# A two-block transformer kernel on one core: a reordered opening, compression products woven between dense ones, and one modulation group moved to the output projection

## The reference, cut to what matters

```python
mod = silu(c) @ w_ada + b_ada                     # 2048 x 12288, one row
shift_m, scale_m, gate_m, shift_f, scale_f, gate_f = split(mod, 6)
h = rms_norm(x, pre_norm_mix) * (1 + scale_m) + shift_m
q, k_c, v_c, ... = split(h @ w_in, ...)
# compression: 32-token blocks of k_c and v_c, each 4096 values -> 128 -> silu -> 128
o = attention(...) @ w_o
x = x + gate_m * rms_norm(o, post_norm_mix)
h = rms_norm(x, pre_norm_ffn) * (1 + scale_f) + shift_f
```

## Time and profile before

| | us |
|---|---|
| median of 3 runs | 2958.68 |
| runs, lowest and highest | 2956.5, 2975.97 |
| the profiled execution | 2958.95 |
| its span, first to last instruction | 2956.8 |
| PE busy, share of the span | 2874.6, 97% |
| DVE busy | 1701.4, 58% |
| ACT busy | 1254.4, 42% |
| mean granted PE clock | 0.983 |

### The profile page before, as it was taken

How to read it: one execution, slowest core, us unless ns; L and a number is a source line. 1 busy time by engine, 2 the same in 40 slices (tenths; PEclk the granted TensorE clock), 3 DMA queues, 4 the chain that set the end, 5 groups by cost and what they waited for, 6 DMA issues and landing times.

```text
span 2956.8 us, 50977 instructions
## 1 busy us (share of the span) xinstructions
PE 2874.6 (97%) x22328; PEld 2652.0 (90%) x22328; DVE 1701.4 (58%) x1507; ACT 1254.4 (42%) x1197; POOL 130.3 (4%) x111
## 2 busy tenths in 40 slices
PE   6999999999999999999999999999999999999998
PEld 5899987799889997899999889999979998899887
DVE  7879877795444454455455654445745554455444
ACT  3334444444434543345343544443345443344333
POOL 0011110000000000000022320000000000000000
PEclk8799999999999999999999999999999999999999
DMA  9999778596556655655452016566554555565553
GB/s 360 388 317 305 268 238 297 176 368 225 186 198 188 197 190 180 203 191 175 157 168 66 10 45 199 187 197 221 178 185 159 197 187 197 187 197 189 181 194 119
DMA packets 300452, 596.72 MB, mean 202 GB/s; under 512 B 12144, under 2 KB 17776, under 8 KB 299760
## 3 DMA queue, kind: packets, MB, share of 16 engines
q1 hardware_dynamic: 294864, 587.83, 59.1%
q10 hardware_dynamic: 5408, 6.23, 0.8%
HBM read 583.80 MB, written 6.29 MB: 200 GB/s over the span
## 4 chain that ended last, share of the span: by engine, by line
PE 83%; DVE 8%; DMA 3%; ACT 3%; issue 2%; POOL 0%; SPq 0%; ACTq 0%; DVEq 0%
PE ps L2429 30%; PE ps L2352 26%; PE ps L2949 9%; PE ps L2534 4%; DVE ada_acc L1593 3%; PE ps L2549 3%; DVE wL L1373 2%; PE ps L3072 2%; DMA ada<-w_ada 2%; PE ps L2830 2%; ACT wH L770 1%; PE ps L2510 1%; DMA raw<-w_up 1%; PE ps L2375 1%; PE ps L2331 0%
## 5 line engine op out<-in xcount | busy, mean ns | idle before, releaser
L1373 DVE TENSOR_TENSOR wL<-raw,wH 128x2048 fp32r<-128x2048 f32 x436 | 1004.3, 2304 | 1064.1 <-ACT wH L770 1060.0
L770 ACT ACTIVATE wH<-raw 128x2048 fp32r<-128x2048 f32 x436 | 837.8, 1922 | 1277.7 <-PE ps L2429 475.4
L2429 PE MATMUL ps<-actH,wH 128*128 128x256 f32 x2816 | 779.3, 277 | 1.7 <-DVE wL L1373 1.6
L2429 PE MATMUL ps<-actL,wH 128*128 128x256 f32 x2816 | 777.7, 276 | 0.0
L2429 PE MATMUL ps<-actH,wL 128*128 128x256 f32 x2816 | 777.7, 276 | 0.0
L2429 PEld LDWEIGHTS ps<-actH,wH 128*128 128x128 f32 x2816 | 529.0, 188 | 3.9 <-DVE wL L1373 2.1
L2429 PEld LDWEIGHTS ps<-actL,wH 128*128 128x128 f32 x2816 | 529.0, 188 | 0.1
L2429 PEld LDWEIGHTS ps<-actH,wL 128*128 128x128 f32 x2816 | 528.9, 188 | 0.0
L2352 PE MATMUL ps<-wH,hidH 128*128 128x512 f32 x1024 | 403.4, 394 | 1.3 <-DVE wL L1373 1.3
L2352 PE MATMUL ps<-wH,hidL 128*128 128x512 f32 x1024 | 400.4, 391 | 0.0
L2352 PE MATMUL ps<-wL,hidH 128*128 128x512 f32 x1024 | 397.4, 388 | 0.0
(11 more groups left out here) (438 smaller groups left out, 3654.6 us busy)
## 6 DMA issues: line engine op xcount, KB each, us to landing
raw<-w_in SPq DMA_DIRECT2D x96, 1024.0 KB, 5.3
ada<-w_ada SPq DMA_DIRECT2D x80, 1024.0 KB, 8.3
raw<-w_up SPq DMA_DIRECT2D x64, 1024.0 KB, 5.4
raw<-w_down SPq DMA_DIRECT2D x64, 1024.0 KB, 5.1
raw<-w_mlp_up SPq DMA_DIRECT2D x64, 1024.0 KB, 5.2
raw<-w_mlp_down SPq DMA_DIRECT2D x64, 1024.0 KB, 5.0
raw<-w_gates SPq DMA_DIRECT2D x48, 1024.0 KB, 5.1
raw<-w_o SPq DMA_DIRECT2D x16, 1024.0 KB, 6.5
```

Of the source, the lines that this page charges most:

```text
L770: nc.scalar.activation(wH[:, s % SPLIT if L[name]["spg"] > 1 else r % SPLIT, :, :], raw[:, slot, :, :], ACT.Copy).then_inc(wh_ready, 1)
L1373: nc.vector.tensor_tensor(wL[:, b, :, :], raw[:, slot, :, :], wH[:, b, :, :].bitcast(F32), ALU.subtract).then_inc(wl_ready, 1)
L2429: ins = nc.tensor.matmul(out, w[:, b, k, cols], v[:, kk, :], start=(kk == 0 and j == 0 and n % 2 == 0), stop=(kk == STEP_K * spg - 1 and j ...
```

## The change

Opening: the squares are taken of the token layout, by ACT with a sum per token, so the root is of a 128x2 tile; PE turns `x` back with a diagonal of the reciprocal roots (32 products into four banks), and ACT copies the normalised `x_f` out. The transfer `gw` is issued after that. Coefficients of c = 1 and 2 are taken one block earlier. For c = 2 and 3 ACT writes `actH` straight from `x_f`, piece by piece, and DVE makes `actL` in four pieces. The first weight tile of quarter 3 is split in halves. `gate_part` goes ahead of the second `front_total`, with two products behind it whose result nobody reads. SP issues the first three weight tiles one block earlier, and tiles 9 to 12 after block 31.

Compression: 24 and 40 of the 64 products are spread between the dense products of steps (1,1) and (1,2). Modulation: group 15 moves from the attention part to `w_o` (32, 16 and 16 blocks).

```diff
-    WIN_ADA = [(2, 0, 0, 1), (1, 1, 3, 4), (1, 1, 0, 1)] + [(2, 1, 0, 1)] * 4 + [(2, 1, 0, 2)]
-    WO_ADA = [(0, 0, 0, 0), (1, 1, 1, 1), (1, 1, 0, 2), (2, 1, 1, 0)]
+    WIN_ADA = [(0, 0, 1, 2), (1, 1, 2, 2), (1, 1, 0, 1)] + [(2, 1, 0, 1)] * 5
+    WO_ADA = [(0, 0, 0, 0), (2, 2, 1, 1), (2, 1, 1, 2), (2, 1, 1, 0)]
...
 # SP
-                    if c == 0 and n >= 5:
-                        weight_block(n - 5)
+                    if c == 0 and n in (4, 5, 6):
+                        weight_block(n - 4)
...
-                    if c == 3 and n == 2:
-                        weight_block(FRONT * c)
+            weight_block(FRONT * 3)
             weight_block(FRONT * 3 + 1)
+            weight_block(FRONT * 3 + 2)
+            weight_block(FRONT * 3 + 3)
             sp.wait_ge(xT_out, 2 * (KT // GT))
...
 # ACT
+                if c == KT // GT - 1:
+                    act.wait_ge(xT_out, n + 1)
+                    chain(nc.scalar.activation(sq_tok[:, t, :], x[:, t, :], ACT.Square, accum_out=rms[:, 1, t:t + 1]))
+            nc.scalar.activation(rms[:, 0, :], rms[:, 1, :], ACT.Sqrt, bias=eps, scale=1.0 / D).then_inc(std_ready, 1)
+            act.wait_ge(low_part, 1)
+            for t in range(TT):
+                ins = nc.scalar.activation(rstd_d[:, t, :], ident, ACT.Identity, scale=rms[:, 2, t:t + 1])
+            ins.then_inc(high_part, 1)
+            for n in range(2 * (KT // GT)):
+                act.wait_ge(xT_done, 2 * (KT // GT) + n + 1)
+                nc.scalar.activation(flat(x_f[:, 2 * n:2 * n + 2, :]), ps[:, n % 4, :], ACT.Copy).then_inc(xT_out, 1)
+            act.wait_ge(xT_out, 4 * (KT // GT))
             act.dma_start(gw[:, :, :], matrix(a["w_gate"])).then_inc(gw_in, 16)
...
 # DVE
+                    if c == 0 and n == 5:
+                        dve.wait_ge(std_ready, 1)
+                        nc.vector.reciprocal(rms[:, 2, :], rms[:, 0, :]).then_inc(low_part, 1)
+                    if c and n == 0:
                         front_coefficients(c - 1)
+                        if c == 3:
+                            first_low(2)
+                            front_split(2, 0)
+                            rest_low(2)
...
+            last_half(slice(0, 2), low_part)
             front_coefficients(3)
+            first_low(3)
+            dve.wait_ge(wh_ready, FRONT * 3 + 1)
+            last_half(slice(2, 4), wl_ready)
+            rest_low(3)
...
 # PE
-                if c < 3:
-                    front_total(2 * c + 3)
                 if c == 0:
                     pe.wait_ge(gw_lo, 1)
                 ins = gate_part(c)
+                if c < 3:
+                    front_total(2 * c + 3)
+                if c < 3:
+                    unread(2)
...
-            compress(0, 22)
-            w_in_step(1, 1)
+            w_in_step(1, 1, compress_between(0, 24))
             pe.wait_ge(vtok_ready, 2)
             score(0)
-            compress(22, 43)
             ada_total(8, 3, 0)
-            w_in_step(1, 2)
-            compress(43, 64).then_inc(cmp_sum, 1)
-            ada_total(9, 3, 0)
+            w_in_step(1, 2, compress_between(24, 2 * CMP_LEN))
             w_in_step(1, 3)
```

More of the change, by code:

```diff
@@ L843, in token_squares @@
                 c = r + i * L.unroll(name)
+                if name == "w_o" and c == 0:
+                    act.wait_ge(ada_rows, 16)
                 for t in range(TT):
@@ L936, in _ @@
             act.wait_ge(consts_in, 48)
-            act.wait_ge(x_in, 16)
-            for c in range(KT // GT):
-                nc.scalar.activation(flat(sq[:, GT * c:GT * (c + 1), :]), flat(x_f[:, GT * c:GT * (c + 1), :]), ACT.Square
-                                     ).then_inc(sq_ready, 1)
-            act.wait_ge(ssum_ready, 1)
-            nc.scalar.activation(std[:, :], ps[:, 6, 0:T], ACT.Sqrt, bias=eps, scale=1.0 / D).then_inc(std_ready, 1)
             for n in range(2 * (KT // GT)):
@@ L957, in _ @@
             for c in range(KT // STEP_K):
+                if c >= 2:
+                    l = FRONT * c
+                    act.wait_ge(raw_in[l % RAW], 16 * (l // RAW + 1))
+                    act.wait_ge(step_done, l + 1)
+                    if c == 2:
+                        nc.scalar.activation(wH[:, l % SPLIT, :, :], raw[:, l % RAW, :, :], ACT.Copy).then_inc(wh_ready, 1)
+                    else:
+                        nc.scalar.activation(wH[:, l % SPLIT, 0:2, :], raw[:, l % RAW, 0:2, :], ACT.Copy).then_inc(high_part, 1)
+                        nc.scalar.activation(wH[:, l % SPLIT, 2:4, :], raw[:, l % RAW, 2:4, :], ACT.Copy).then_inc(wh_ready, 1)
+                    act.wait_ge(coef_ready, c + 1)
+                    act.wait_ge(act_ready, 2 * (c - 1))
+                    for k in range(GT):
+                        n = GT * c + k
+                        ins = nc.scalar.activation(actH[:, n, :], x_f[:, n, :], ACT.Identity, bias=mod[:, 0, n:n + 1],
+                                                   scale=cf(0)[:, n:n + 1])
+                        if k:
+                            ins = nc.scalar.activation(yf[:, c % 2, k, :], x_f[:, n, :], ACT.Identity, bias=mod[:, 0, n:n + 1],
+                                                       scale=cf(0)[:, n:n + 1])
+                        if k % 2:
+                            ins.then_inc(h_ready, 1)
+                        else:
+                            ins.then_inc(high_part, 1)
+                    act.sem_inc(y_ready, 2)
+                    front_split(c, 1)
+                    front_split(c, 2)
+                    continue
                 front_split(c, 0)
@@ L1649, in front_coefficients, with piece_low, first_low, rest_low @@
                                                ).then_inc(coef_ready, 1)
+            def piece_low(c, k):
+                n = GT * c + k
+                nc.vector.tensor_tensor(actL[:, n, :], yf[:, c % 2, k, :], actH[:, n, :].bitcast(F32), ALU.subtract
+                                        ).then_inc(act_ready if k % 2 else low_part, 1)
+            def first_low(c):
+                n = GT * c
+                dve.wait_ge(coef_ready, c + 1)
+                link(nc.vector.tensor_scalar(yf[:, c % 2, 0, :], x_f[:, n, :], cf(0)[:, n:n + 1], mod[:, 0, n:n + 1], ALU.mult, ALU.add))
+                dve.wait_ge(high_part, 2 if c == 2 else 5)
+                piece_low(c, 0)
+            def rest_low(c):
+                dve.wait_ge(h_ready, 2 * c + 1)
+                piece_low(c, 1)
+                dve.wait_ge(high_part, 3 if c == 2 else 6)
+                piece_low(c, 2)
+                dve.wait_ge(h_ready, 2 * c + 2)
+                piece_low(c, 3)
             for c in range(KT // STEP_K):
@@ L2447, in _ @@
             pe.wait_ge(consts_in, 48)
-            for _ in range(4):
+            for _ in range(2):
                 nc.tensor.matmul(ps[:, 4, :], ident, common[:, 0:4 * P], start=True, stop=True)
-            for c in range(KT // GT):
-                pe.wait_ge(sq_ready, c + 1)
-                for k in range(GT * c, GT * (c + 1)):
-                    ins = nc.tensor.matmul(ps[:, 6, 0:T], ones, sq[:, k, :], start=(k == 0), stop=(k == KT - 1))
-            ins.then_inc(ssum_ready, 1)
+            pe.wait_ge(x_in, 16)
             for n in range(2 * (KT // GT)):
```

147 lines of the change are left out of this document (84 added, 63 removed).

## The result

The changed kernel takes 2996.85 us (median of 4 runs, 2992.58 to 3007.91) against 2965.04 for the kernel before beside it: 1.0119 times as long, 95% interval 1.0100 to 1.0139 (the ratio on record; the quotient of these two medians is 1.0107). The prediction, 2952 in a range of 2938 to 2963, forecast a gain where there is a loss. The profiled execution after took 2992.58 us with a span of 2990.8, which is 34.0 more than the span before.

What follows compares the result with a forecast made beforehand. PE, busy 97% of the span, was taken as the bound, with DVE fullest in the opening. Gains of 8.2, 4.0 and 2.4 less 7.5 gave 7.1 us off 2958.95: 2952 us, range 2938 to 2963.

Steps and rivals of the forecast that it cites:

- gain 8.2: Opening, up to the first w_in step: would end at 155.7 instead of 163.85 us; bounds 3 and 11.
- gate weights that hold the first quarter: Rival for the opening: gw and the first pieces come late, gain only 3 us, time 2957; chance 0.14.
- at about 35.5: Opening: when ACT would issue the gw load after eight copies, instead of at 29.9 us.
- minus some 1.3 of DVE's 5.7 us of waiting for ACT, as coefficients come a block earlier: Opening, up to block 31: earlier coefficients would save DVE some 1.3 us of waiting.
- my 155.7: End of the opening: forecast start of w_in in us, where the kernel before has 163.85.
- The walk's waits: Groups 0 and 1 of w_in: queue walk-through gave waits of 3.5 us at (1,0) and 2.9 at (1,1).
- I take all: Woven compression, 205 to 241 us: all 8.6 us lost to the low clock would come back.
- The mix is 60% dense in time: Woven compression: share of dense products, given as reason that the clock keeps 1.00.
- I cost it at nothing: Group 2: one more modulation block of 2.7 us, costed at zero because DVE is about 3.7 us ahead.
- gain 2.4: Rest of attention: the last block no longer delays the first w_o split, saving 2.4 us; bounds 0 and 13.
- 7.5: w_o with 16 blocks instead of 12: a loss of 7.5 us; bounds a gain of 3 and a loss of 20.
- `w_o` eats it all: Rival for w_o: blocks land in 9.5 us instead of 7.0, w_o costs 20 us, time 2964; chance 0.14.

Runs made afterwards that it cites:

- e10: Changed kernel with gate weights loaded early and coefficients and splits of quarters 2 and 3 one modulation block later on DVE; w_in starts at 159.1 us.
- e11: Changed kernel with all repairs: gate weights, coefficients, GpSimd issuing compression weights, blocks 32 and 33 earlier, slots, group 16's total; ratio 1.0017 to the kernel before.
- e2: Changed kernel with the opening of the kernel before, all else of the diff kept; up_0 starts 26.8 us later than in the kernel before.
- e5: Kernel before with only the modulation group moved to w_o (32/16/16 tables); up_0 starts 25.6 us later than in the kernel before.
- e3: Kernel before with only the weaving of compression products into steps (1,1) and (1,2); ratio interval 1.0003 to 1.0025.
- e8: Changed kernel with ten instead of eight w_in modulation blocks alternating in slots 4 and 5; group 2 to w_o takes 195.9 us instead of 202.8.
- e7: Changed kernel with PE's total of modulation group 16 one w_o step sooner; w_o takes 8.2 us less than in the changed kernel.
- e1: Kernel before with the changed opening alone and its own order of later loads; w_in starts at 168.3 us, up_0 12.4 us later than before.
- e9: Changed kernel with the four compression weight loads issued by GpSimd instead of SP; ratio 1.0136, group 2 starts 6.0 us sooner than in the changed kernel.
- e14: e11 with three slots instead of two for w_o's modulation blocks; w_o takes 110.7 us, up_0 starts at 555.3 us.
- e12: Kernel before, own modulation tables, with repaired opening, weaving and GpSimd issuing compression weights; up_0 at 557 us or later, w_o takes 104.7 us.
- e13: e11 with the compression weights issued by SP in the order of the kernel before; group 1 starts 0.9 us and group 2 17.1 us later than in e11.
- e6: Changed kernel with modulation blocks 32 and 33 ahead of the compression weights, those ahead of two tiles; group 2 starts 9.9 us later than in the changed kernel.

## Why the prediction was wrong

The terms of the sum against what the traces of before and after show at the same places, as gains:

```
                         forecast   measured
opening                     8.2       -6.5
w_in to group 2             4.0       -5.1
group 2                     0        -10.3
group 3 to w_o              2.4        0.0
w_o                        -7.5      -13.3
sum                         7.1      -35.2
```

**The opening, "gain 8.2".** The loss measured is 6.5. The rival was right in its mechanism, gate weights that hold the first quarter, and its price (gain 3) was far off. The term that failed is "at about 35.5": I took eight copies at 0.6 us each from the earlier trace rows, but a copy waits for PE's four products ahead of it: the first stands at 32.4 and the rest follow at a pitch of 0.9 us or more, behind PE's 8.87. `gw` was issued at 39.8. Next, "minus some 1.3 of DVE's 5.7 us of waiting for ACT, as coefficients come a block earlier" has the wrong sign: at the two places that were moved a block earlier, DVE waits 4.3 and 1.9 us for PE's columns, where the kernel before has no wait over 0.3, and e10 gains 2.8 by undoing it. DVE was done with block 31 at 142.0 instead of 131. Without both mistakes `w_in` starts at 156.9 (e11) to 159.1 (e10), against my 155.7; what is left is in the terms up to block 31, which DVE ends at 132.5 and 134.6: the first quarter starts 0.4 and 0.6 us sooner than in the kernel before, not 3. (The terms named for the last stretch add up to 155.3, not 155.7.)

**The order of SP's loads, not costed.** The prediction moves SP's queue in words ("SP issues 34 only after DVE has done 32") and prices no load that was moved past the start of `w_in`. Behind those of `cw1` SP stands for 8.6 to 11.1 us each. The walk's waits, 3.5 before step (1,0) and 2.9 before (1,1), were 11.2 and none, and 2.1 before (0,3). This is the step that failed in "group 1"; its end, group 2 at 229.5, is what e11 nearly reaches (232.9). Of this loss little is left at `up_0` once the moved group is in (e2 against e5).

**The weaving, "I take all".** The clock did what was forecast, 1.00 in the woven steps. The sum was wrong: 8.6 us of clock in a stretch were credited in full, with DVE 30.89 of 36 us busy in the same row and blocks 9.5 us on their way. Alone it gave nothing (e3). "The mix is 60% dense in time" holds for group 1 as a whole; in the two woven steps the dense products are 11.2 of 25.4 us, 44%.

**Group 2's extra block, "I cost it at nothing".** Group 2 took 10.3 us longer, of which 6.9 are the slot (e8) and up to 3.4 remain, near the 2.7 of the block itself. I counted DVE's lead and not the block's slot, whose place in SP's list is behind two later blocks and a tile.

**The rest of the attention part, "gain 2.4".** From group 3 to `w_o` after takes 161.1 us and before 161.2: nothing.

**`w_o`, "7.5".** 13.3 were lost. One total in the wrong place in PE's list, whose wait the walk didn't have, is some 6 of them (mean of eight traces 122.0, of the three without it 115.8). Without it the loss is 5.1 (e7) and 6.9 (e11) against the kernel before, and 9.8 between the means (115.8 and 106.0), so the term itself was of the right size. Blocks landed in 5.8 us in the median, not 7.0, so the rival "`w_o` eats it all" had the right stage and the wrong reason.

So the losses are mostly orders in a queue: an issue behind copies, loads ahead of tiles, a block behind later blocks, a total behind a step. With all of them put right (e11) the change still costs 3.7 us at `up_0` instead of gaining 7.1.

## What to carry to other kernels

When a change moves an instruction that frees something (a slot, an accumulator, a column of totals), follow the loop to its end: who waits for it, and what is queued behind that waiter. If what is queued there feeds the engine that owns the instruction, the loop closes, and the cost is a whole step, not the instruction.

A stretch at a low clock is worth nothing by itself. Ask when the other engines would let PE go on; undo one part alone before crediting it. Transfers of many small rows belong where no other queue needs to issue.

## What the runs showed of the hardware

- A load in 512-byte rows (2 MB in 4096 of them) that nothing slow precedes issues in 0.9 to 2.9 us, but the next load of SP then stands for 8.6 to 13.1 us in its queue (before, after, e1). When GpSimd issued the rows, a later issue of SP stood for 10.4 (e9), 11.5 (e11) and 12.4 us (e14). 1 MB tiles or blocks issued among them landed after 23.3 us (e14) and 26.5 (e12).
- PE stayed at the lower of its two clocks, 1.2 GHz (granted 0.50), for 21 us (e13) and 15 us (e6) without idle time in between, in a mix of dense products and narrow ones that ran at 2.4 GHz (1.00) in twelve other traces. In e6 it fell to the lower one while PE was busy at the higher.
